# A two-block transformer kernel on one core: stick-breaking sums added up by VectorE, an earlier first matmul in the normed stages, and two reorderings

## The reference

```
for layer in range(2):
    proj = rms_norm(x, mix_norm_g) @ w_in
    y_a = diff_attention(...)        # 4 heads, 128 wide
    y_b = stick_breaking(...)        # 4 heads, 64 wide
    y_c = latent_attention(...)      # 4 heads; q, k and v from normed latents
    x = x + concat([y_a, y_b, y_c]) @ w_out
    x = x + memory_attention(rms_norm(x), mem)
    x = x + square(relu(rms_norm(x) @ w_ff1)) @ w_ff2
```

```
z = q @ k.T * SB_DIM ** -0.5
log_beta = log_sigmoid(z)
log_1m_beta = where(earlier, log_sigmoid(-z), 0)
later = cumsum(log_1m_beta, axis=3, reverse=True) - log_1m_beta
a = where(earlier, exp(log_beta + later), 0)
```

## Time and profile before

| | |
|---|---|
| median of 3 runs | 2730.33 us (2725.55 to 2733.7) |
| profiled execution | 2732.64 us, its span 2730.9 us |
| TensorE busy | 2612.0 us, 96% of the span |
| VectorE, ScalarE, GpSimd busy | 41%, 26%, 48% |
| mean granted clock of TensorE | 0.979 |
| chain that ended last | PE 67%, DVE 2%, ACT 2% of the span |

### The profile page before, as it was taken

One profiled execution on the slowest core, in us unless ns is written; L12 is line 12 of the kernel. 1 busy time (PEld: TensorE's weight loads), 2 busy tenths in 40 slices (PEclk: granted clock), 3 DMA queues, 4 the chain that ended last, 5 costly groups with the idle time before them and its releaser, 6 DMA issues.

```text
span 2730.9 us, 35326 instructions
## 1 busy us (share of the span) xinstructions
PE 2612.0 (96%) x14617; PEld 2088.5 (76%) x14617; DVE 1127.2 (41%) x1948; ACT 696.4 (26%) x1360; POOL 1308.7 (48%) x544
## 2 busy tenths in 40 slices
PE   7998899999999988999999899899999999999998
PEld 6876567888888765678888766688888787788887
DVE  3343364666532433546666434422222234422224
ACT  4244452111122344421111234310001333300002
POOL 5442135665565421355555553366556431356653
PEclk9999899999999998999999999999999999999999
DMA  7310024555332100145554210222232210132231
GB/s 239 88 57 32 16 63 138 182 185 186 125 106 80 57 32 16 63 134 170 185 186 143 70 58 32 88 93 92 93 107 92 78 63 32 53 102 93 92 104 65
DMA packets 222509, 265.34 MB, mean 97 GB/s; under 512 B 19249, under 2 KB 197001, under 8 KB 222249
## 3 DMA queue, kind: packets, MB, share of 16 engines
q1 hardware_dynamic: 219648, 256.56, 29.0%
q10 hardware_dynamic: 2728, 6.90, 0.7%
HBM read 258.72 MB, written 4.72 MB: 96 GB/s over the span
## 4 chain that ended last, share of the span: by engine, by line
PE 67%; DVE 2%; ACT 2%; POOL 0%; issue 0%; PEldq 0%; DVEq 0%; PEld 0%; ACTq 0%
PE PS L946 8%; PE PS L949 8%; PE PS L950 8%; PE PS L912 4%; PE PS L916 4%; PE PS L917 4%; PE PS L1630 2%; PE PS L1634 2%; PE PS L1633 2%; PE PS L1908 1%; PE PS L1961 1%; PE PS L930 1%; PE PS L1784 1%; PE PS L1753 1%; PE PS L933 1%; PE PS L934 1%
## 5 line engine op out<-in xcount | busy, mean ns | idle before, releaser
L824 POOL TENSOR_SCALAR WH<-RAW 128x2048 fp32r<-128x2048 f32 x178 | 341.4, 1918 | 1183.4 <-issue 1032.2
L826 POOL TENSOR_TENSOR WL<-RAW,WH 128x2048 fp32r<-128x2048 f32 x178 | 821.6, 4616 | 14.8
L946 PE MATMUL PS<-Hh,WL 128*128 128x512 f32 x1152 | 448.6, 389 | 0.0
L949 PE MATMUL PS<-Hl,WH 128*128 128x512 f32 x1152 | 448.2, 389 | 0.0
L950 PE MATMUL PS<-Hh,WH 128*128 128x512 f32 x1152 | 448.2, 389 | 0.0
L2577 DVE SCALAR_TENSOR_TENSOR X<-PS,X 128x512 f32<-128x512 f32 x304 | 208.8, 689 | 226.0 <-PE PS L1634 137.0
L950 PEld LDWEIGHTS PS<-Hh,WH 128*128 128x128 f32 x1152 | 216.3, 188 | 45.1
L946 PEld LDWEIGHTS PS<-Hh,WL 128*128 128x128 f32 x1152 | 216.3, 188 | 45.1 <-issue 0.4
L949 PEld LDWEIGHTS PS<-Hl,WH 128*128 128x128 f32 x1152 | 216.3, 188 | 44.6
L2934 DVE TENSOR_TENSOR PS<-SQ,PS 128x512 f32<-128x512 f32 x44 | 30.6, 696 | 436.9 <-PE PS L950 436.9
L1630 PE MATMUL PS<-U,WL 128*128 128x512 f32 x512 | 202.8, 396 | 3.6 <-DVE X L2577 3.6
(11 more groups left out here) (521 smaller groups left out, 4772.5 us busy)
## 6 DMA issues: line engine op xcount, KB each, us to landing
RAW<-in_w_ff SPq DMA_DIRECT2D x64, 1024.0 KB, 5.4
PROJ<-in_ada_w SPq DMA_DIRECT2D x48, 1024.0 KB, 8.0
RAW<-in_ffn_w_in SPq DMA_DIRECT2D x44, 1024.0 KB, 5.0
RAW<-in_ffn_w_out SPq DMA_DIRECT2D x22, 1024.0 KB, 4.8
RAW<-in_w_in SPq DMA_DIRECT2D x20, 1024.0 KB, 5.3
RAW<-in_w_out SPq DMA_DIRECT2D x8, 1024.0 KB, 4.9
RAW<-in_a_w_in SPq DMA_DIRECT2D x6, 1024.0 KB, 5.0
RAW<-in_b_w_in SPq DMA_DIRECT2D x12, 512.0 KB, 4.5
```

The lines of the kernel that those rows point to most:

```text
L824: pool.tensor_scalar(WH[b][:, :], RAW[b][:, :], 1.0, 1.0, ALU.mult, ALU.mult).then_inc(s.split_hi, 1)
L826: pool.tensor_tensor(WL[b][:, :], RAW[b][:, :], WH[b][:, :].bitcast(F32), ALU.subtract).then_inc(s.split_done, 1)
L946: ins = mm(bank, WL[b][:, col:col + P], Hh[:, k, :], start=k == 0, stop=False)
L949: mm(bank, WH[b][:, col:col + P], Hl[:, k, :], start=False, stop=False)
```

## The change

It has four parts. **First**, `panel_k` waits for k + 1 normed tiles where it waited for at least two. **Second**, in the mixing stage only the first two token spreads stand in front of the key products; the third and fourth stand in front of the first and second value product, and ScalarE's evictions are put in a matching order. **Third**, in `sb_rest` the sums over later blocks are formed on 128 columns each: the neighbouring block's part is multiplied straight from its softplus, and the others, where several later blocks act on the same queries, are first added up by VectorE, three adds a head into PTS or SQ, counted by `mix.sp` (now eight a pair in place of two). The own-block products come first. **Fourth**, the spread of the window sums leaves `pt`; as `sums_spread` it runs at the end of the same iteration, behind the dense steps and pv(p - 3).

```diff
@@ -649,6 +649,11 @@
             at = 1280 * hh + sb_off[hh][j]
             return PS[:, :, :].rearrange("p a n -> p (a n)")[:, at:at + S - P * j]
 
+        def sb_later(hh):
+
+            y = (SQ if hh else PTS)[:, 0, :]
+            return y[:, 0:P], y[:, P:2 * P], y[:, 2 * P:3 * P]
+
         def sb_head(x, hh):
             return x[:, 1280 * hh:1280 * hh + 1280]
 
@@ -924,7 +929,7 @@
                 begin(at)
                 pe.wait_ge(s.g_evac, g + 2)
                 for k in range(KT):
-                    pe.wait_ge(ready, count + max(k + 1, 2))
+                    pe.wait_ge(ready, count + k + 1)
                     for j in range(2):
                         bank, col = PS[:, bank0 + j, :], k * 256 + j * P
                         ins = mm(bank, WL[b][:, col:col + P], Hh[:, k, :], start=k == 0, stop=False)
@@ -1302,13 +1307,14 @@
                     ins = mm(bank[:, P * c:P * c + P], kv_root[:, c:c + 1].to_broadcast([P, P]), ident, start=True, stop=True)
                 ins.then_inc(s.f_tile, 1)
                 pe.wait_ge(mix.r, tn + TN_YA + 1)
-                for x in range(4):
+                for x in range(2):
                     token_spread(feed(1 + x), TN_YA, 2 * x, P)
 
                 pe.wait_ge(s.f_evac, emptied(0))
                 for tp in range(2):
                     up(3 + tp, 1, lambda k: Hh[:, 4, :], lambda k: Hl[:, 4, :], 768 + P * tp)
                 for j in range(2):
+                    token_spread(feed(3 + j), TN_YA, 4 + 2 * j, P)
                     pe.wait_ge(s.g_evac, gu + 5 + j + 1)
                     fill_s((5 + j) % BANKS, (2 * j, 2 * j + 1), 256, [0],
                            lambda W, k: W[b][:, 1024:1280],
@@ -1331,17 +1337,23 @@
 
                 def sb_rest(tp, hh):
                     it = L * 2 + tp
-                    pe.wait_ge(mix.sp, it * 2 + hh + 1)
-                    for j in (0, 1, 3, 2):
-                        if j == 2:
-                            if hh:
-                                pe.wait_ge(mix.a, it * 2 + 1)
-                            else:
-                                pe.wait_ge(mix.sp, it * 2 + 2)
-                        z = ZP(hh, j)
-                        ins = mm(z, ntri, SP(hh, j), start=False, stop=j == QT - 1, skip_group_check=True)
-                        for jj in range(j + 1, QT):
-                            ins = mm(z[:, P * (jj - j):], nones, SP(hh, jj), start=False, stop=jj == QT - 1, skip_group_check=True)
+                    pe.wait_ge(mix.sp, it * 8 + hh + 1)
+                    for j in (0, 1, 3):
+                        mm(ZP(hh, j), ntri, SP(hh, j), start=False, stop=j == QT - 1, skip_group_check=True)
+                    if hh:
+                        pe.wait_ge(mix.a, it * 2 + 1)
+                    else:
+                        pe.wait_ge(mix.sp, it * 8 + 2)
+                    mm(ZP(hh, 2), ntri, SP(hh, 2), start=False, stop=False, skip_group_check=True)
+                    mm(ZP(hh, 2)[:, P:2 * P], nones, SP(hh, 3), start=False, stop=True, skip_group_check=True)
+                    for j in range(2):
+                        mm(ZP(hh, j)[:, P:2 * P], nones, SP(hh, j + 1)[:, 0:P], start=False, stop=False, skip_group_check=True)
+                    last, *both = sb_later(hh)
+                    pe.wait_ge(mix.sp, it * 8 + 3 + 3 * hh)
+                    mm(ZP(hh, 1)[:, 2 * P:3 * P], nones, last, start=False, stop=True, skip_group_check=True)
+                    for x in range(2):
+                        pe.wait_ge(mix.sp, it * 8 + 4 + 3 * hh + x)
+                        ins = mm(ZP(hh, 0)[:, P * (x + 2):P * (x + 3)], nones, both[x], start=False, stop=x == 1, skip_group_check=True)
                     ins.then_inc(mix.rs, 1)
 
                 def sb_values(tp):
@@ -1762,6 +1774,8 @@
                     for c in range(k1 - k0):
                         ins = pe.transpose(PS[:, 3 + hh, c * P:c * P + P], win_p(p, hh)[:, 1 + c * P:1 + c * P + P], ident)
                     ins.then_inc(wa.pt, 1)
+            def sums_spread(p):
+
                 if p % QT == QT - 1:
                     pe.wait_ge(wa.r, p // QT + 1)
                     pe.wait_ge(wa.pc[0], win_copied(p) - 1)
@@ -1799,6 +1813,8 @@
                     next(x)
                 if p >= 3:
                     pv(p - 3)
+                if 2 <= p < WIN_PAIRS + 2:
+                    sums_spread(p - 2)
 
             begin(PN_A + 8)
             pe.wait_ge(wa.m, 2 * WIN_PAIRS)
@@ -2284,19 +2300,19 @@
                     taken(tp, q_nope[:, tp, :], sq_ml[tp]).then_inc(s.g_evac, 1)
                 act.wait_ge(mix.kv_n, L + 1)
                 f(Hh[:, 4, :], PS[:, 6, :], ACT.Copy).then_inc(mix.kv_hi, 1)
-                for k in range(2):
-                    high(k)
+                high(0)
                 act.wait_ge(s.g_tile, gu + 3)
                 square(sq_ml[2], PS[:, 2, :])
                 f(q_rope, PS[:, 2, :], ACT.Copy, scale=PC[:, K_ROPEQ, L, :]).then_inc(s.g_evac, 1)
+                high(1)
+                for tp in range(2):
+                    taken(3 + tp, k_nope[:, tp, :], sq_ml[4 + tp]).then_inc(s.g_evac, 1)
+                high(2)
+                taken(5, mlv[:, 0:2, :]).then_inc(s.g_evac, 1)
                 square(sq_ml[3], PROJ[:, 15, :])
                 f(k_rope, PROJ[:, 15, :], ACT.Copy, scale=PC[:, K_ROPEK, L, :]).then_inc(mix.rope, 2)
-                for k in range(2, 4):
-                    high(k)
-                for tp in range(2):
-                    taken(3 + tp, k_nope[:, tp, :], sq_ml[4 + tp]).then_inc(s.g_evac, 1)
-                for j in range(2):
-                    taken(5 + j, mlv[:, 2 * j:2 * j + 2, :]).then_inc(s.g_evac, 1)
+                high(3)
+                taken(6, mlv[:, 2:4, :]).then_inc(s.g_evac, 1)
 
                 psf = PS[:, :, :].rearrange("p a n -> p (a n)")
 
@@ -2785,6 +2801,14 @@
                         v.wait_ge(mix.x, it * 6 + 4 + hh + 1)
                         y = sb_head(ATT, hh)
                         v.scalar_tensor_tensor(y, sb_head(psf, hh), 0.0, y, ALU.max, ALU.add).then_inc(mix.sp, 1)
+                    for hh in range(2):
+                        last, *both = sb_later(hh)
+                        if hh == 0:
+                            v.wait_ge(mix.sp, it * 8 + 2)
+                        v.tensor_tensor(last, SP(hh, 2)[:, P:2 * P], SP(hh, 3), ALU.add).then_inc(mix.sp, 1)
+                        v.tensor_tensor(both[0], SP(hh, 1)[:, P:2 * P], SP(hh, 2)[:, 0:P], ALU.add).then_inc(mix.sp, 1)
+                        v.wait_ge(mix.sp, it * 8 + 3 + 3 * hh)
+                        v.tensor_tensor(both[1], SP(hh, 1)[:, 2 * P:3 * P], last, ALU.add).then_inc(mix.sp, 1)
 
                 softplus(0)
                 for i in range(3, 6):
```

## The result

| | before | after |
|---|---|---|
| median of 4 runs each | 2732.01 us (2725.55 to 2741.85) | 2689.42 us (2684.74 to 2699.81) |
| ratio, 95% interval | | 0.9842 (0.9815 to 0.9869) |
| later medians | 2736.1 us, 63 runs (2722.1 to 2743.7) | 2699.2 us, 13 runs (2684.6 to 2706.9) |
| profiled execution, its span | 2732.64, 2730.9 us | 2686.82, 2685.0 us |
| mean granted clock | 0.979 | 0.989 |

A forecast was written before the change was run, and what follows sets the result against it. TensorE was taken as the bound: its few waits for VectorE or ScalarE and its streamed columns. Gains 5.8 + 6.0 + 6.9 + 8.3 = 27.0 us gave 2705.6 from the profiled 2732.6, 2703.3 against the median; range 2695 to 2714.

The forecast's parts named there:

- the 3.55: Second layer's mixing stage: gain in us from the new order, expecting full clock and 3.11 us from fourth spread to scores.
- the upper bound of 4.05: Second layer's mixing stage: gain in us if the clock does not fall and the third spread is quicker by 0.5.
- TensorE stood 1.14 us in front of it: Window stage: TensorE's wait before the sums' spread; seven such waits and a last of 0.35 go, 8.3 us.
- the last wait's 0.35: Window stage: the eighth wait before a spread of the sums, 0.35 us, counted as saved within the 8.3.
- everything behind each place being matmul time that moves along: Behind all four changed places: later work shifts along, so the gains sum to 27.0 us.
- the clock's 4 us either way: Four late stage starts: chance in when TensorE's clock rises can add or take up to 4 us.
- (a): Window stage: ScalarE's copy over 0.96 us late, next transposes wait, that stage's gain all lost; 2711.6 us, chance 0.10.
- (b): Mixing stage: ScalarE delivers tile 2 late, VectorE's chain slips, the new order gives nothing; 2709.3 us, chance 0.07.
- (c): Stick-breaking sums: late adds or waits between small products leave about 3 of 6.9 us; 2707 us, chance 0.07.
- (d): Window stage: ScalarE, held at the spread's copy, misses exponentials, eight turns lost, 32 us; slower, 2743.6 us, chance 0.02.

The follow-up runs named there:

- f3: Kernel before, with twelve unneeded filler products in TensorE's 1.9 us wait ahead of each latent attention's second unit; 2726.9 us, ratio 0.9958.
- f2: The changed kernel, unchanged, run again for a second profile; 2704.3 us, ratio 0.9860.
- f1: The kernel before, unchanged, run again for a second profile; 2736.0 us, ratio 1.0012.
- e2: Only the mixing stage's new order of spreads, products and evictions, on the kernel before; 2729.3 us, ratio 0.9959.
- i1: Changed kernel with fillers sized to waits in stick-breaking, latent and memory attention, plus eight in each of four late norm waits; 2676.8 us, ratio 0.9793.

## Why the prediction was wrong, point by point

What a stage took from its first instruction to the next stage's, in us, mean over the profiles without fillers that have the part and over those that don't, and the shortest of each:

| stretch, part | without | with | difference | of the shortest | forecast |
|---|---|---|---|---|---|
| last feed-forward and first late start, 1 | 413.9 | 413.0 | 0.9 | 1.2 | 1.3 |
| three more late stages, 1 | 989.7 | 984.5 | 5.2 | 5.3 | 4.0 |
| mixing to scores, first layer, 2 | 23.5 | 20.4 | 3.1 | 2.5 | 2.45 |
| the same, second layer, 2 | 24.5 | 20.3 | 4.3 | 1.8 | 3.55 |
| heads, first layer, 3 | 63.5 | 61.1 | 2.4 | 3.4 | 3.5 |
| heads, second layer, 3 | 63.8 | 59.2 | 4.6 | 5.0 | 3.5 |
| window stage, 4 | 147.4 | 136.6 | 10.8 | 10.7 | 8.3 |

The sum of the means is 31.2 us, and with 0.2 at each mixing layer's start 31.6, against 27.0. What is there with TensorE at full clock is less: 4 x 1.32 + 2 x 0.20 us of part 1, 2 x 2.46 of part 2, 8 x 0.84 of part 3 and 10.8 of part 4, together 28.1. The stretches that the change doesn't touch differ little: the latent stretch of the first layer has 70.4 us in the mean without and 70.6 with the whole change, that of the second 70.6 and 68.0, the memory stages 0.2 and 0.1 less. The 13.3 us in the first two profiles were luck.

- **Part 1** was right: the late starts gave 6.1 us for 5.3, the first matmul moving by 1.32 us at each, and the two mixing layers gave 0.2 each for 0.27. The prediction read half clock at two of the four starts; the profile of before has it at all four. Behind the first matmuls it comes to 18 us before and 16 after, so the rise of the clock did move along with the start.
- **Part 2** was right in the first layer to the hundredth (2.46 us at full clock). In the second the 3.55 stood for one execution in which a spread ran at half clock; over the profiles it is 4.3, just above the upper bound of 4.05. There the five profiles with the part all have 3.4 us at half clock in this stage, the six without it 3.4 to 17.1, in the mean 10.8.
- **Part 3** was right: 0.84 a head for 0.87 at full clock, adds of 0.28 us as in the earlier trace rows, no gap in any head of the three profiles of the changed kernel.
- **Part 4** had its mechanism right and its size wrong. "TensorE stood 1.14 us in front of it" is the term: it stood 1.38, and the new order saves 0.16 more. 7 x 0.40 = 2.8 us, of which the last wait's 0.35 came back ahead of line 1826. The Trainium skill, "Perfetto Trace Analysis", "Tensor Engine Instruction (MATMUL, LD_WEIGHTS)", says that the profiler estimates TensorE's end times from the size of the instruction; the 0.60 against 0.36 us agree.
- **The step that failed** is "everything behind each place being matmul time that moves along". Matmul time doesn't simply move along: the same matmuls take half the time when the clock is up, and a fall of the clock can start from a wait (f3). I looked at the clock at the late starts and in one spread, "the clock's 4 us either way", and not in the stages between, where the profile of before had 20 us at half clock per layer. The work itself was forecast within 1.1 us (28.1 for 27.0, part 4 up and part 2 down); the term put at nothing, the clock, is the other 9 of the 37.0 us: 3.5 within the table's stages and 5.4 beyond it, of which the untouched stages of the profiles show 3. Changed runs had a mean clock of 0.979 to 0.989, before 0.974 to 0.983. f3 shows that a fall can start from a wait, but that wait is the same in both kernels. That the change shortens waits in the mixing stages and at the late starts, and so spares falls, fits the half clock counted in part 2's stage; no run isolates it, for parts 2 and 3 least of all, so the cause of this clock gain is argued and stays open.
- **The range**, 2695 to 2714, missed the first median and holds the pooled 2699.2, but that by luck: it stood for gains of 16 to 35 us from 2730.3, the pooled median of before is 2736.1, and the pooled gain of 37.0 lies outside. It took the scatter from three runs of before (8 us); 63 show 21.6, and the changed kernel has 22. No rival came true: none of the waits (a), (b), (c) or (d) named appeared.

Open is how much of the 37 belongs to the clock. The comparison at an equal mean clock says 24 to 26 us of work, the places at full clock 28, the stages 31; the first rests on one to three runs of the changed kernel at each clock.

## What to carry to other kernels

Before an estimate, list the stretches in which TensorE's granted clock is low and the wait in front of each: a wait of 1.9 us cost 1.9 us and behind it from nothing to 7 us more, in the mean 5. Measure both kernels several times before a few us are explained: the largest difference between the first two profiles was a draw. Where the wait can't be removed, fill it with matmuls into a free bank, and count their passes, so that they end before the wait does. Size an idle time of TensorE from start to start of matmuls, not from the modelled end.

## What was not expected of the hardware

The same program, with the same data, spread by 22 us (0.8%) over 13 executions, and as much over the four of f2; two of its profiles differ by 20 us, with 62 and 113 us at half clock. Behind one wait of 1.94 us the granted clock was at 0.50 for 20 us; behind the same wait in f1 for 10, and in e2's first layer it did not fall. The Trainium skill, "TensorE: Matmul & The Clock Gate", Part 1, puts the cost of warming up, told for a kernel's start, under 1% of a typical span. Here the clock fell 16 times in the profile of before, and its 119 us at half clock are up to 60 us of 2731, 2.2%; i1 took back 22 us of after's 2699. For falls that come again the measurement decides. And a product of two fp32 identities shows as two records of 0.12 us, so a filler cost twice what I first took.
